# Hybrid GDN, MLA and MoE step on one core: experts 1 to 3 and tiles 8 to 23 written out ahead of the loop, not experts 29 to 31 and the last tiles behind it

## The reference

```
logits = h @ w_router + b_router            # 32 experts, top 4 of each token, softmax over the 4
for each expert e, its rows xb:
    gu  = xb @ w_gu[e] + b_gu[e]            # w_gu[e]: 1024 x 2048 f32
    gt  = min(gu[:, :1024], 7);  up = clip(gu[:, 1024:], -7, 7)
    act = gt * sigmoid(1.702 * gt) * (up + 1)
    y   = act @ w_down[e] + b_down[e]       # w_down[e]: 1024 x 1024 f32
    x[token] += gate[token, e] * y
```

## Time and profile before

| | us |
|---|---|
| median of three executions | 1343.31 |
| the profiled execution's own time | 1344.16 |
| its span | 1342.2 |
| PE busy in the span | 1285.6 (96%) |
| DVE busy | 459.4 (34%) |
| ACT busy | 215.1 (16%) |

### The profile page before, as it was taken

The page is one execution under the profiler, slowest core; times in us unless marked ns, Lnnn a source line. Parts: engine busy times, 40 slices in busy tenths (PEclk is TensorE's granted clock), DMA queues, the critical chain, the costliest instruction groups (busy, mean ns, idle before and its releaser), DMA issues.

```text
span 1342.2 us, 20973 instructions
## 1 busy us (share of the span) xinstructions
PE 1285.6 (96%) x8616; PEld 586.4 (44%) x8616; DVE 459.4 (34%) x977; ACT 215.1 (16%) x573; POOL 20.6 (2%) x28
## 2 busy tenths in 40 slices
PE   5999999899999999999999999999999999999997
PEld 4577645467645333333333343333433333333332
DVE  2364234442546223333233332233322322332223
ACT  3451333550232000000000000000000000000000
POOL 0000001100000000000000000000000000000000
PEclk9999999889998999999999999999999999999999
DMA  9511010464208999999999999999999999999996
GB/s 339 205 63 65 2 29 16 165 232 200 79 7 344 428 426 428 426 429 429 428 429 430 426 429 429 429 428 429 430 426 429 429 428 429 429 427 428 427 428 250
DMA packets 48051, 440.60 MB, mean 328 GB/s; under 512 B 7635, under 2 KB 10169, under 8 KB 23334
## 3 DMA queue, kind: packets, MB, share of 16 engines
q1 hardware_dynamic: 47916, 439.90, 78.7%
q10 hardware_dynamic: 90, 0.06, 0.0%
HBM read 436.62 MB, written 3.33 MB: 328 GB/s over the span
## 4 chain that ended last, share of the span: by engine, by line
PE 71%; DMA 20%; SPq 3%; DVE 2%; ACT 2%; issue 1%; POOL 0%; DVEq 0%; ACTq 0%
PE bank L1047 69%; DMA weights<-in_w_gu 15%; SPq L417 3%; DMA small_weights<-in_w_gu 3%; PE bank L1050 2%; DMA gain_cols<-in_norm_ffn 1%; ACT scaled L608 1%; DMA weights<-in_w_mq 1%; POOL stats L580 0%; PE bank L1679 0%; DVE x L2373 0%; DVE x L2218 0%; ACT stream L608 0%; ACT small_weights L608 0%; DVE weights L1805 0%
## 5 line engine op out<-in xcount | busy, mean ns | idle before, releaser
L1047 PE MATMUL bank<-weights,small_weights 128*64 128x512 f32 (+3 forms) x1632 | 376.3, 589 | 7.4 <-DMA weights<-in_w_gu 7.4
L2373 DVE SCALAR_TENSOR_TENSOR x<-bank,small_weights,x 128x512 f32<-128x512 f32 (+1 forms) x192 | 134.8, 744 | 604.0 <-PE bank L1047 604.0
L1047 PEld LDWEIGHTS bank<-weights,small_weights 128*64 128x64 f32 (+1 forms) x1632 | 117.5, 138 | 224.9 <-issue 188.8
L1047 PE MATMUL bank<-weights,scaled 128*64 128x512 f32 x768 | 170.1, 595 | 6.1 <-ACT scaled L608 6.1
L608 ACT ACTIVATE scaled<-bank 128x256 f32<-128x256 f32 (+5 forms) x153 | 58.1, 407 | 323.8 <-PE bank L1047 240.8
L1047 PE MATMUL bank<-scaled,small_weights 64*128 64x512 f32 x384 | 108.1, 640 | 1.4 <-DVE x L2373 0.7
L608 ACT ACTIVATE scaled<-scaled 128x512 f32<-128x512 f32 x32 | 20.2, 630 | 555.0 <-DVE scaled L1809 555.0
L1047 PE MATMUL bank<-small_weights 128*64 128x512 f32 (+2 forms) x488 | 105.6, 514 | 1.2 <-DVE small_weights L1805 0.6
L1047 PEld LDWEIGHTS bank<-weights,scaled 128*64 128x64 f32 x768 | 53.7, 137 | 106.0 <-issue 98.8
L1047 PE MATMUL bank<-small_weights,weights 128*128 128x320 f32 (+3 forms) x320 | 86.5, 420 | 0.9 <-ACT small_weights L608 0.9
L1047 PEld LDWEIGHTS bank<-stream 128*128 128x128 bf16 (+1 forms) x2416 | 74.9, 99 | 28.0 <-issue 26.4
(11 more groups left out here) (191 smaller groups left out, 851.3 us busy)
## 6 DMA issues: line engine op xcount, KB each, us to landing
weights<-in_w_gu SPq DMA_DIRECT2D x96, 2048.0 KB, 27.4
weights<-in_w_down SPq DMA_DIRECT2D x48, 2048.0 KB, 27.8
stream<-in_w_gu SPq DMA_DIRECT2D x16, 2048.0 KB, 26.6
small_weights<-in_w_gu SPq DMA_DIRECT2D x16, 2048.0 KB, 27.4
stream<-in_w_down SPq DMA_DIRECT2D x8, 2048.0 KB, 29.9
small_weights<-in_w_down SPq DMA_DIRECT2D x8, 2048.0 KB, 30.2
weights<-in_w_in SPq DMA_DIRECT2D x4, 2048.0 KB, 14.3
stream<-in_w_out SPq DMA_DIRECT2D x2, 2048.0 KB, 10.6
```

The costliest lines, as they stand in the source:

```text
L1047: return pe.matmul(out, lhsT, rhs, start=start, stop=stop)
L2373: dve.scalar_tensor_tensor(xx, PS[bank][0:rows, :], gcur[0:rows, b:b + 1], xx, ALU.mult, ALU.add)\
```

## The change

The same experts and tiles are worked on in the same order by the same instructions. What moves is the border between the loop and what is written out. On SP, tiles 8 to 23 are written out ahead of the loop, and the loop does tiles 24 to 191. On PE, experts 1, 2 and 3 are written out ahead of the loop, and the loop does experts 4 to 31. Both loops still have seven turns. `FIRST` is the first expert of the loop.

```
-        GT, TILES, SLOTN, TURN = 4, 6, 8, 4
+        GT, TILES, SLOTN, TURN, FIRST = 4, 6, 8, 4, 4
...
         def turned(i, c):
             return [(ap, name, i * (16 * TURN * TILES // SLOTN) + count)
-                    for ap, name, count in (tile_at(TILES * (1 + c) + t) for t in range(TILES))]
+                    for ap, name, count in (tile_at(TILES * (FIRST + c) + t) for t in range(TILES))]
...
-            with sp.Fori(0, (E - 2) // TURN) as i:
-                for n in range(SLOTN, SLOTN + TURN * TILES):
-                    refill(n, i)
-            for n in range(SLOTN + (E - 2) // TURN * TURN * TILES, E * TILES):
+            for n in range(SLOTN, FIRST * TILES):
                 sp.wait_ge(sem("tile_used"), n - SLOTN + 1)
                 dst, name, _ = tile_at(n)
                 sp.dma_start(dst, tile_rows(n // TILES, n % TILES, True)).then_inc(sem(name), 16)
+            with sp.Fori(0, (E - FIRST) // TURN) as i:
+                for n in range(FIRST * TILES, (FIRST + TURN) * TILES):
+                    refill(n, i)
...
-            with pe.Fori(0, (E - 2) // TURN) as i:
+            for e in range(1, FIRST):
+                expert(e, fixed(e))
+            with pe.Fori(0, (E - FIRST) // TURN) as i:
                 for c in range(TURN):
-                    expert(i * TURN + (1 + c), turned(i, c))
-            for e in range(1 + (E - 2) // TURN * TURN, E):
-                expert(e, fixed(e))
+                    expert(i * TURN + (FIRST + c), turned(i, c))
```

## The result

The changed kernel took 1370.95 us (median of six, 1363.31 to 1381.77), the kernel before 1343.70 beside it: 1.0201 times, interval 1.0157 to 1.0245, some 27 us slower. I had forecast 1353, with an upper end of 1361. The direction and the fetches of code are as forecast, the size isn't.

What follows compares the result with a forecast made beforehand. The weight stream on DMA was taken to bound the kernel; -0.2 us (SyncE) and +10.1 us (code fetches) made +9.9, a median of 1353.2 us, with PE's branch waits hidden; range 1342.5 to 1361.

Steps and rivals of the forecast that it cites:

- What bounds the kernel: The weight stream's start, 4.89 us a tile and the tail set the end; PE has 11.8 us to spare, DMA none.
- SyncE's part: Tiles 8 to 23 written out on SyncE: the first refill is issued earlier, -0.2 us; other tiles hidden by queued transfers.
- the written-out experts: Experts 1 to 3 written out on PE: same matmuls, turn-end gaps hidden by the DMA queue, 0 us.
- the loop's end: PE's loop exit before the last scatters: 0 us behind the queue, 0.1 if that cover were gone.
- nine blocks through eight places: In PE's instruction memory, a turn asks for nine code blocks, eight are held: nine fetches a turn, 54 in six turns.
- The rivals with 12 more fetches or none: PE's code: 12 fetches on one engine, 1361.1 us, chance 0.10; spread, 1345.4, 0.14; code still fits, 1343.1, 0.30.
- The alignment: PE's new loop begins at 245 in its code block and ends at 1836, 44 instructions into an 8th block.
- The price at the branch: PE's back branch waits for its block: 1.5 us a turn, 9 in all, inside PE's 11.8 us to spare.
- Fetches as load on the DMA engines, +10.1 us,: 54 code fetches over eight DMA engines in turn, 1.5 us each, slow the weight stream by 10.1 us.
- The sum: Whole kernel: -0.2 + 10.1 = +9.9 us, 1353.2 us for a median.
- Two of the prediction's signs: In the profile after: periods of 117.4 us a turn become some 119, and 424 GB/s in place of 428.
- The sign that belongs to the stream: In the weight stream, landing times of the last tiles grow turn by turn.

Runs made afterwards that it cites:

- experiment 5: The changed kernel with 60 instructions that do nothing added at PE's start: 1346.71 us, 0.9998 times the kernel before.
- experiment 6: The kernel before with SyncE's half of the change alone (tiles 8 to 23 written out), PE as before: 1345.09 us, 0.9997.
- experiment 3: The kernel before with 116 instructions that do nothing added at PE's start: 1342.59 us, 0.9959.
- experiment 8: The kernel before with 60 instructions that do nothing added at PE's start: 1345.35 us, 0.9988.
- experiment 10: The kernel before with 26 idle instructions added in each expert of PE's loop: 1344.51 us, 1.0000.
- experiment 4: The changed kernel with PE's loop written out in full, SyncE's loop kept: 1349.36 us, 1.0014 times the kernel before.
- Experiment 7: The changed kernel with tiles 8 to 191 transferring only 512 of 4096 columns, PE working on stale weights: 1342.11 us in one execution.
- the first experiment: The changed kernel with 30 instructions that do nothing added at PE's start: 1389.98 us, 1.0306.
- experiment 2: The kernel before with 146 instructions that do nothing added at PE's start: 1365.56 us, 1.0114.
- experiment 12: The kernel before with 133 idle instructions added at PE's start: 1353.13 us, 1.0059.
- experiment 9: The changed kernel as it is, measured and profiled again: 1370.44 us, 1.0208.

## Why the prediction was wrong

**What bounds the kernel** held: the undisturbed stream sets the end of before, and PE's spare time was 13.5 us where I took 11.8. I counted some ten experts from the first wait for a transfer on, where eleven run behind 1001 us, and left out the 1.2 us by which the last three were slower.

**SyncE's part, the written-out experts, the loop's end:** as forecast, nothing (experiments 5 and 6). The forecast of 0.2 us is below what could be seen.

**Code: nine blocks through eight places.** Right, and to the packet: 54 more, nine a turn. The rivals with 12 more fetches or none are out. That eight is the most held, and that the oldest goes first, no row of before shows; the sum took both as given. The runs bear both out. What needs eight blocks has no q8 packet between the first branch and the last (before and experiments 3, 5, 6, 8 and 10, 33 or 34 packets on the page), what needs nine has nine a turn (87 or 88 on the page), so none of the nine was still there when its turn came. A return over seven blocks of body that were held took 0.21 us. For the size of a block I had 20 packets for 5011 instructions, about 250 each; I took 256. In experiment 4 the 23 packets that start from 463.12 to 861.77 us come 18.45 us apart (a straight line through their starts) while an expert's 390 instructions take 28.21, which makes 255.

**The alignment** was right for the changed kernel by luck of the margin. The loop begins at about 220 of its block and not at 245, and both lie in the bad zone of 202 to 255 (a body of 1591 instructions fits seven blocks from 201 or less). To get from a packet's time to a place in the program I took three things: that the fetch is asked for just as the engine enters a block, that the sequencer was 30 to 40 instructions ahead (one window, has 38), and "about 1 us (some 10 instructions)" for the fetch to come on its way, for which I had no row. Experiment 7, where hardly a transfer is under way at the branch, as before just ahead of 420 us (no packet of any queue from 647.8 to 648.8 us, two from 418.5 to 419.9), shows 1.0 to 1.6 us at the branch and 0.7 to 1.3 us at the next block; at the 10 instructions a us of the earlier trace rows (26 and 24 in 5 us) that is 7 to 16 instructions. Together the three put the boundary some 25 instructions too early. The third makes up 3 of them at most; which of the others has the rest, no run shows. The same error made the first experiment miss by 47 us.

**The price at the branch is the step that failed.** "I take 1.5, so 9 us in all, inside PE's 11.8 us to spare"; my ends were 0 to 4.3 us a turn. It was 6.4, and four things make it up. The wait was 6.1 us, 2.1 us of it beyond what PE's queue covered; I had a code packet's 1.2 us and a tile's 7.8 as the nearest rows and took 1.5 net of the queue. Of the 6.1 us, 2.4 came with the weight stream and 3.7 stand without it (experiment 7). The target block was not the only one missing: with 36 instructions in the first block the engine ran dry again before the next had come, 2.3 us (experiments 1, 2 and 12 show how this follows the place). After the two holes TensorE was granted 0.52 of its clock for 3.4 us, 1.6 us more. And 0.4 us lie in the pieces around the holes. I had none of the last three.

**Fetches as load on the DMA engines, +10.1 us,** is of the right kind and size (experiment 4: 6 us expected, 5.9 found, for 36 packets more, which would be 8.9 for 54). That eight engines take them in turn, at 1.5 us each, was not tested by itself. That a tile needs all 16 engines, and so waits for the one with most fetches, fits what was measured: a tile is carried by all of them (experiment 7), and 36 packets of 1.2 us shared evenly by 16 engines would have cost 2.7 us and not 5.9. But the term lies off the path: the prediction put the fetches in the sum and hid the branches behind PE's spare time, and it was the other way round. With 24.9 us lost at the branches beyond that spare time, PE was later than the stream, and the fetches were the hidden part.

**The sum:** 38.4 at the branches less 13.5 to spare is +24.9; the medians differ by 27, and single executions differ by more than that gap in their start alone. Two of the prediction's signs came true for another reason: turns of some 119 us and slices under 424 GB/s were to be the slower stream, and are PE's holes. The sign that belongs to the stream, landing times that grow, failed: they fell from 27 to 17 us.

## What to carry to other kernels

The cost of a loop of this size depends on where it lies: seven blocks of body and one behind it fitted here (34 packets, 1342.6 us with N = 116), and 17 instructions more ahead of the loop broke that (88 packets, 1353.1 us with N = 133). Count the body's instructions and look at the code queue's packets: none in steady turns was the sign that it fits, nine a turn that it doesn't; there, some idle instructions ahead of the loop, at a place where the engine waits anyway, undid the loss (experiment 5, 1346.71 against 1370.95 us). And where a bound engine and a nearly bound one share a cost, price both and take the larger sum.

## What the hardware showed that I had not expected

- A taken branch to a block that is not held takes 6.1 us while the weight stream runs, 3.7 us with the stream cut to an eighth, 0.21 us where the block is held. The block behind it lets PE go on 5.2 to 6.0 us after PE's first matmul in the first.
- 17 and 13 more instructions of no work at PE's start moved the kernel before from 1342.6 to 1353.1 and to 1365.6 us (N = 116, 133, 146).
- Two holes of 2.0 and 2.6 us within 8 us were followed by 3.4 us at a granted TensorE clock of 0.52, and so (0.51 to 0.59) at all six returns of the profiled changed kernel but not at each in experiment 9 (1.00 behind the third). One hole can do it too, but doesn't always: in experiment 12 the clock fell behind single holes of 2.76, 2.31 and 1.95 us, and stayed at 1.00 behind holes of 2.06, 2.09 and 2.14.
- The stream's start varies by 13 us between executions of one kernel (423.35 and 434.91 us). The granted clock from 250 to 300 and 300 to 350 us was 0.73 and 0.90 with the late one, 0.86 and 1.00 with the other.
